# ScalarE issues the stores of the expert results, and SyncE runs on into the next layer's loads

## The chip, the cores and the metric

The kernel runs on one NeuronCore of one Trainium2 chip. The metric is the device time of one execution in microseconds (us), from three executions of the kernel before. Engines are called PE (TensorE, matrix products), DVE (VectorE), ACT (ScalarE), POOL (GpSimd) and SP (SyncE). SP computes nothing: it issues loads and stores to the 16 DMA engines. "PEq", "ACTq", "SPq" and "POOLq" are the sequencers of these engines, which issue DMAs and handle registers, branches and semaphores.

## What is computed

Two encoder layers over 512 tokens (two groups of 256) of width 1024, then a final norm. Of a layer only the second half matters here:

```python
h2 = rms_norm(x, norm_ffn) * (1 + scale2) + shift2
x = x + gate2 * grouped_moe(h2, w_router, router_bias, w_gate, w_up, w_down)

def grouped_moe(h, w_router, router_bias, w_gate, w_up, w_down):
    ...
    for e in range(N_EXPERTS):                      # 16 experts, 2 of them for each token
        a = jax.nn.silu(t @ w_gate[e]) * (t @ w_up[e])
        out = out + gate[:, e:e + 1] * (a @ w_down[e])
```

The first half of a layer starts with the modulation `silu(c) @ w_ada`, a norm of x, and the projection with `w_in`. All values are fp32.

## The kernel before

**The expert stage.** Each token's row is copied to a DRAM buffer (`rows_by_expert`) at the places of its two experts. The buffer is cut into tiles of 128 rows that belong to one expert. In this run each layer has 16 tiles. They are handled in pairs (`par` 0 and 1): a hardware loop over 7 pairs (`rest`), and a last pair written out behind it. For each tile, three weights of 2 MB (gate, up, down) and 0.5 MB of rows are loaded, and a result of 0.5 MB (`y_row[:, par, :]`) is stored back to its place in the buffer. The weights live in six slots of SBUF (`ring0` to `ring5`), three for each `par`. A product is made in three passes: ACT writes a rounded copy of half a weight (`high`, L1291, 128x2048), DVE subtracts it from the weight (`low`, L1835), and PE multiplies high by high, high by low and low by high (L943 to L945 for gate and up, L958 to L960 for down). Such a half weight is a "part"; six parts make a tile, and the semaphore `part_used` counts the parts that PE has finished.

**The order on each engine is written out by hand.** On PE, tile n takes: turning the next tile's rows (L923), its own two up parts, the next tile's first gate part, turning its own activations (L931), the next tile's second gate part, and its two down parts. L931 waits for DVE's product of silu and up (L1861). On ACT, tile n takes: the next tile's rows rounded (`rows_high`, L1298), silu (L1312), the next tile's second gate part, two down parts, the turned activations rounded (L1319), two up parts, the first gate part of the tile after the next, and last the two copies of the result from PSUM to `y_row` (L1328), which raise `y_ready`. Then the next tile's L1298 follows.

**SP.** For each tile `expert` (L638 on) loads the rows and the three weights of the tile two further on, each as soon as `part_used` says that its slot has been used up. The last load, of down, waits for the tile's last part. Then SP waits for `y_ready` and issues the store (L648). Behind both last tiles SP waits until the stores have landed (`y_stored`) and raises `tiles_stored`. Only then does SP enter the next pass of the layer loop.

**Between the layers.** POOL waits for `tiles_stored` (L1940), then gathers the rows from the buffer with 8 indirect DMAs (L1943). All engines meet at a barrier (`arrived`, `go`) which POOL's arrival completes. In the new layer, SP loads in the order of `BLOCKS`: `ada0`, `ada1`, `qa` (2 MB in 8 DMAs of 256-byte pieces), `ada2`, `ada3`, and so on. For the first block in each slot it waits for a count of `part_used` that says when the slot's last expert weight was used (L585); `LAST_PARTS` holds how many parts before the stage's end that is: 12 for `ada0`, 8 for `ada1`, 4 for `qa`, 6 for `ada2`, 0 for `ada3`. Before the load of `ada3` it waits until the gather is complete. PE multiplies `ada0` and `ada1` (L716), ACT copies the products (L1125) and then weighs the gathered rows (L1091), DVE adds the second expert's rows (L1508), PE turns the sums (L748), and DVE adds them to x (L1500). Behind the second layer the same steps L1091 to L1500 follow, without any load of weights.

Of the kernel before, what the change touches and what calls it, by code (L numbers as in the profile page):

```python
# [29 lines left out]
P = 128  # L30
# [6 lines left out]
DEPTH = 2  # L37
# [15 lines left out]
MAX_TILES = 2 * TOK // P + NE  # L53
# [35 lines left out]
PARTS_BEFORE = 16  # L89
# [209 lines left out]
def build_trunk(nc, t_in, y_prompt, y_sample):  # L299
# [7 lines left out]
    with ctx:  # L307
# [3 lines left out]
        def sem(name):  # L311
            return ctx.enter_context(nc.semaphore(name))


        rows_dram = nc.dram_tensor("rows_by_expert", (TILE_ROWS, D), F32, kind="Internal").ap()
# [51 lines left out]
        y_row = part(10240, 2048).rearrange("p (b d) -> p b d", b=2)  # L367
# [47 lines left out]
        plan_i = sb("plan_i", [1, 4 + MAX_TILES], I32)  # L415
# [18 lines left out]
        S = {n: sem(n) for n in names}  # L434
# [7 lines left out]
        xg_landed = [sem(f"xg_landed{par}") for par in range(2)]  # L442
        rows_sent = sem("rows_sent")
        rows_out = sem("rows_out")
        tiles_stored = sem("tiles_stored")
        got_rows = [sem(f"got_rows{t}") for t in range(TT)]
        arrived = sem("arrived")
        go = sem("go")
# [2 lines left out]
        passed = sem("passed")  # L451
        xgT_done = sem("xgT_done")
# [4 lines left out]
        part_used = sem("part_used")  # L457
# [5 lines left out]
        y_ready = sem("y_ready")  # L463
        y_stored = [sem(f"y_stored{par}") for par in range(2)]
# [73 lines left out]
        def _(sp):  # L538
# [36 lines left out]
            with sp.Fori(0, DEPTH) as layer:  # L575
# [39 lines left out]
                def expert_of(tile):  # L615
                    return sp.value_load(plan_i[0:1, bass.ds(tile + 4, 1)], min_val=0, max_val=NE - 1)

                def load_weights(k, e, par):
                    name = ("w_gate", "w_up", "w_down")[k]
                    sp.dma_start(ring[EXPERT_SLOTS[par][k]][:, :].rearrange("p (k n) -> p k n", k=(KC, KC, FC)[k]),  # L620
                                 t_in[name][bass.ds(layer, 1), bass.ds(e, 1), :, :]
                                 .rearrange("o e (k p) n -> p (o e k) n", p=P))\
                      .then_inc(w_landed[par][k], 16)

                def load_rows(tile, par):
                    sp.dma_start(xg[:, par, :], rows_dram[bass.ds(tile * P, P), :]).then_inc(xg_landed[par], 16)
# [6 lines left out]
                load_rows(0, 0)  # L633
                load_rows(1, 1)

                def expert(p, par, last=False):
                    n = (done_before + p) * 2 + par
                    tile = p * 2 + par  # L638
                    at = (done_before + p) * 12 + 2 + 6 * par
                    if not last:  # L640
                        e = expert_of(tile + 2)
                        sp.wait_ge(xgT_done, n + 1)
                        load_rows(tile + 2, par)
                        for k, after in enumerate((0, 2, 6)):
                            sp.wait_ge(part_used, PARTS_BEFORE + at + after)
                            load_weights(k, e, par)
                    sp.wait_ge(y_ready, n + 2)
                    sp.dma_start(rows_dram[bass.ds(tile * P, P), :], y_row[:, par, :]).then_inc(y_stored[par], 16)  # L648

                with sp.Fori(0, rest) as p:  # L650
                    for par in range(2):
                        expert(p, par)
                for par in range(2):
                    expert(rest, par, last=True)
                for par in range(2):
                    sp.wait_ge(y_stored[par], (done_before + rest) * 16 + 32)
                nc.sync.sem_inc(tiles_stored, 1)

            for t in range(TT):
                sp.wait_ge(y_rows_a, t + 1)  # L660
# [358 lines left out]
        def _(act):  # L1019
# [109 lines left out]
            with act.Fori(0, DEPTH) as layer:  # L1129
# [172 lines left out]
                def expert(p, par, last=False):  # L1302
# [24 lines left out]
                    for half in range(2):  # L1327
                        ins = nc.scalar.copy(y_row[:, par, half * 512:(half + 1) * 512], bank[2 + half][:, :])  # L1328
                    ins.then_inc(y_ready, 1)

                for h in range(2):
                    high(0, 0, 0, h, h, before * 12 + h)
# [568 lines left out]
        def _(pool):  # L1901
# [6 lines left out]
            with pool.Fori(0, DEPTH) as layer:  # L1908
# [26 lines left out]
                pool.wait_ge(rows_sent, layer * (32 * TT) + 32 * TT)  # L1935
                nc.gpsimd.sem_inc(rows_out, 1)

                pool.wait_ge(tiles_stored, layer + 1)
                nc.gpsimd.sem_inc(passed, 1)
                nc.gpsimd.drain().then_inc(arrived, 1)  # L1940
                for t in range(TT):
# [32 lines left out]
```

## Time and profile before

| | us |
|---|---|
| median of 3 runs | 1858.26 |
| lowest, highest | 1854.97, 1861.24 |
| the profiled execution, its own time | 1855.56 |
| its span, first to last instruction | 1853.7 |
| PE busy, DVE busy, ACT busy | 1525.7, 1042.1, 884.7 |

Around the span lie 1.9 us. The profiled execution is 2.7 us faster than the median. The busy times are sums over stages with different limits. The two expert stages run from about 558 to 912 us and from about 1452 to 1803 us.

### The profile page before, as it was taken

Reading aid. Unit: us, or ns where it says so; the run is one execution under the profiler, and the core shown is the slowest. Engines: PE = TensorE matmul, PEld = TensorE weight load, DVE = VectorE, ACT = ScalarE, POOL = GpSimd, SP = SyncE. Lnnn points to the kernel's source line nnn. Section 1 sums busy time; section 2 is a strip of 40 time slices with the busy share of each in tenths; the row PEclk is TensorE's granted clock in tenths of the full one; section 3 lists DMA queues with packets and bytes.
Section 4 is the critical chain, followed back from the end, with each engine's and each line's share of the span. In section 5 each row is a group of like instructions: output and inputs, shape, how many; then the busy total and the mean of one; then the engine's idle time right before and its main releaser. Section 6 shows DMA issues by size and latency. Waiting matters only on the chain.

```text
span 1853.7 us, 18702 instructions
## 1 busy us (share of the span) xinstructions
PE 1525.7 (82%) x6462; PEld 1090.4 (59%) x6462; DVE 1042.1 (56%) x1320; ACT 884.7 (48%) x1146; POOL 46.7 (3%) x45
## 2 busy tenths in 40 slices
PE   4799987999836999999569999699995389999974
PEld 2377545666614777777337664366672277777753
DVE  2654468223345777777353735932245387777744
ACT  2532357112225777777254324721123377777743
POOL 2001000000010000000100000000000000000001
PEclk9899998999967999999779999899997699999996
DMA  8629660112246999999392147011123789899933
GB/s 244 210 91 354 224 194 1 46 58 79 84 182 223 342 351 355 347 358 358 128 332 91 68 159 251 23 46 46 46 91 120 276 319 358 322 353 355 359 124 134
DMA packets 169107, 375.27 MB, mean 202 GB/s; under 512 B 22438, under 2 KB 25136, under 8 KB 168912
## 3 DMA queue, kind: packets, MB, share of 16 engines
q1 hardware_dynamic: 157792, 339.75, 51.3%
q0 software_dynamic: 8176, 31.46, 4.6%
q10 hardware_dynamic: 3072, 3.19, 0.6%
q8 instruction: 38, 0.62, 0.1%
q14 instruction: 29, 0.24, 0.0%
HBM read 333.49 MB, written 40.89 MB: 202 GB/s over the span
## 4 chain that ended last, share of the span: by engine, by line
PE 54%; DMA 15%; ACT 9%; issue 9%; DVE 8%; SPq 2%; ACTq 1%; POOL 1%; DVEq 0%; POOLq 0%
DMA ring<-in_w_gate 10%; PE bank L685 8%; PE bank L687 8%; PE bank L686 8%; PE bank L880 6%; PE bank L716 2%; PE bank L958 2%; PE bank L960 2%; PE bank L959 2%; PE bank L833 2%; PE bank L855 2%; PE bank L943 2%; PE bank L944 2%; ACT x_lo L1291 2%; PE bank L945 2%
## 5 line engine op out<-in xcount | busy, mean ns | idle before, releaser
L685 PE MATMUL bank<-x_hi,w_lo 128*128 128x512 f32 x608 | 259.2, 426 | 20.7 <-DVE x_lo L1448 9.0
L1291 ACT CAST x_lo<-ring 128x2048 fp32r<-128x2048 f32 x96 | 183.5, 1913 | 123.2 <-issue 56.8
L687 PE MATMUL bank<-x_hi,w_hi 128*128 128x512 f32 x608 | 239.9, 394 | 0.0
L686 PE MATMUL bank<-x_lo,w_hi 128*128 128x512 f32 x608 | 239.3, 394 | 0.0
L1835 DVE TENSOR_TENSOR w_lo<-ring,zone_r 128x2048 fp32r<-128x2048 f32 x92 | 210.4, 2289 | 28.3 <-ACT zone_r L1291 28.2
L1291 ACT CAST zone_r<-ring 128x2048 fp32r<-128x2048 f32 x96 | 181.6, 1912 | 19.9 <-PE bank L960 14.3
L943 PE MATMUL bank<-w_lo,zone_r 128*128 128x512 f32 x384 | 164.9, 429 | 5.2 <-issue 5.2
L685 PEld LDWEIGHTS bank<-x_hi,w_lo 128*128 128x128 f32 x608 | 115.5, 190 | 63.3 <-issue 30.2
L1425 DVE TENSOR_TENSOR w_lo<-ring,w_hi 128x1024 fp32r<-128x1024 f32 x84 | 102.0, 1220 | 85.1 <-ACT w_hi L1084 84.5
L1835 DVE TENSOR_TENSOR w_lo<-ring,x_lo 128x2048 fp32r<-128x2048 f32 x36 | 82.4, 2292 | 113.4 <-ACT x_lo L1291 113.4
L686 PEld LDWEIGHTS bank<-x_lo,w_hi 128*128 128x128 f32 x608 | 116.0, 191 | 31.7 <-issue 9.6
L687 PEld LDWEIGHTS bank<-x_hi,w_hi 128*128 128x128 f32 x608 | 115.6, 190 | 25.5
L1247 ACT ACTIVATE zone<-bank 128x512 f32<-128x512 f32 x32 | 19.1, 597 | 217.8 <-PE bank L687 217.8
L880 PE MATMUL bank<-zone,ring 128*128 128x512 f32 x256 | 115.8, 595 | 0.9
L944 PE MATMUL bank<-x_lo,zone_r 128*128 128x512 f32 x272 | 115.5, 425 | 0.0
L945 PE MATMUL bank<-x_lo,zone_r 128*128 128x512 f32 x272 | 114.9, 422 | 0.0
L1084 ACT CAST w_hi<-ring 128x1024 fp32r<-128x1024 f32 x84 | 87.1, 1044 | 22.4 <-PE bank L687 6.1
L923 PE MATMUL bank<-const,zone 128*128 128x128 f32 x256 | 35.0, 282 | 74.3 <-DMA zone<-rows_by_expert 74.3
L945 PE MATMUL bank<-zone_r 128*128 128x512 f32 x240 | 94.6, 394 | 0.0
L944 PE MATMUL bank<-zone_r 128*128 128x512 f32 x240 | 94.6, 394 | 0.0
L943 PEld LDWEIGHTS bank<-w_lo,zone_r 128*128 128x128 f32 x384 | 78.3, 204 | 22.4 <-issue 6.0
L1835 DVE TENSOR_TENSOR w_hi<-ring,x_lo 128x2048 fp32r<-128x2048 f32 x32 | 73.3, 2293 | 26.4 <-ACT x_lo L1291 26.4
(242 smaller groups left out, 2590.8 us busy)
## 6 DMA issues: line engine op xcount, KB each, us to landing
ring<-in_w_gate SPq DMA_DIRECT2D x32, 2048.0 KB, 13.5
ring<-in_w_up SPq DMA_DIRECT2D x32, 2048.0 KB, 15.7
ring<-in_w_down SPq DMA_DIRECT2D x32, 2048.0 KB, 8.8
ring<-in_w_ada SPq DMA_DIRECT2D x24, 2048.0 KB, 9.1
ring<-in_w_in SPq DMA_DIRECT2D x14, 2048.0 KB, 7.9
zone<-rows_by_expert SPq DMA_DIRECT2D x32, 512.0 KB, 8.7
rows_by_expert<-zone SPq DMA_DIRECT2D x32, 512.0 KB, 8.7
rows_by_expert<-zero_row POOLq DMA_DIRECT2D x4, 3072.0 KB, 28.8
```

Source lines behind the costliest of these rows:

```text
L685: mm(out, lo, x_first, start=start, stop=False)
L686: mm(out, hi, x_second, start=False, stop=False)
L687: return mm(out, hi, x_first, start=False, stop=stop)
L716: ins = mm(ps[32 * j:32 * (j + 1), :], cs[:, k, :], w[:, k, :], start=(k < 4), stop=(k >= KC - 4))
L880: ins = mm(ps[:, :], w[:, k, j * P:(j + 1) * P], oT[:, k, :], start=(k == 0), stop=(k == 3))
L943: mm(out, xg_hi[:, par, c, :], wv[:, c, :], start=(c == 0), stop=False)
L944: mm(out, xg_lo[:, par, c, :], hi[:, k, :], start=False, stop=False)
L945: ins = mm(out, xg_hi[:, par, c, :], hi[:, k, :], start=False, stop=(c == KC - 1))
L1084: nc.scalar.copy(w_hi[:, n % W_BUFS, :, :], group_view(ring[SLOT[b]], b, c)).then_inc(S["w_hi_ready"], 1)
L1291: nc.scalar.copy(part_hi[buf], ring[EXPERT_SLOTS[par][k]][:, h * 2048:(h + 1) * 2048])\
L1425: v.tensor_tensor(group_view(w_lo[SLOT[b]], b, c), group_view(ring[SLOT[b]], b, c), w_hi[:, n % W_BUFS, :, :].bitcast(F32), ALU.subtract). ...
L1835: v.tensor_tensor(w_low[EXPERT_SLOTS[par][k]][:, cols], ring[EXPERT_SLOTS[par][k]][:, cols], part_hi[buf].bitcast(F32), ALU.subtract)\
```

## The change

ACT itself waits for `y_ready` behind its two copies and issues the store. SP no longer waits for `y_ready`, issues no store, and has no pass for the two last tiles, since they had nothing but the store. SP also no longer waits for `y_stored`. POOL waits for both `y_stored` semaphores, with the number of pairs read from the plan, before it gathers. Nothing else is changed.

```diff
                 def expert(p, par):
...
-                    if not last:
-                        e = expert_of(tile + 2)
...
+                    e = expert_of(tile + 2)
+                    sp.wait_ge(xgT_done, n + 1)
+                    load_rows(tile + 2, par)
+                    for k, after in enumerate((0, 2, 6)):
+                        sp.wait_ge(part_used, PARTS_BEFORE + at + after)
+                        load_weights(k, e, par)
-                    sp.wait_ge(y_ready, n + 2)
-                    sp.dma_start(rows_dram[bass.ds(tile * P, P), :], y_row[:, par, :]).then_inc(y_stored[par], 16)
...
-                for par in range(2):
-                    expert(rest, par, last=True)
-                for par in range(2):
-                    sp.wait_ge(y_stored[par], (done_before + rest) * 16 + 32)
-                nc.sync.sem_inc(tiles_stored, 1)
...
                     for half in range(2):
                         ins = nc.scalar.copy(y_row[:, par, half * 512:(half + 1) * 512], bank[2 + half][:, :])
                     ins.then_inc(y_ready, 1)
+                    act.wait_ge(y_ready, n + 2)
+                    nc.scalar.sem_inc(passed, 1)
+                    act.dma_start(rows_dram[bass.ds((p * 2 + par) * P, P), :], y_row[:, par, :])\
+                       .then_inc(y_stored[par], 16)
...
-                pool.wait_ge(tiles_stored, layer + 1)
+                pool.wait_ge(S["plan_ready"], 1)
+                pairs_done = pool.value_load(plan_i[0:1, 1:2], min_val=0, max_val=DEPTH * MAX_TILES // 2)
+                for par in range(2):
+                    pool.wait_ge(y_stored[par], pairs_done * 16 + 16)
                 nc.gpsimd.sem_inc(passed, 1)
```

On ACT, at the end of the loop's second tile, before (the buffer `zone` is `y_row` at L1328, `bank2` and `bank3` hold the result, L1337 is the loop's branch):

```order
L1325 REGISTER_ALU
L1328 COPY zone<-bank2 128x512 [waits y_stored1,part_used]
L1328 COPY zone<-bank3 128x512
L1337 REGISTER_ALU
L1337 COMPARE_AND_BRANCH
L1296 ISA
L1298 CAST zone_r<-bank4 128x512 [waits xgT_done]
```

and now, at the same place, where the lines are 5 to 9 lower:

```order
L1316 REGISTER_ALU
L1319 COPY zone<-bank2 128x512 [waits y_stored1,part_used]
L1319 COPY zone<-bank3 128x512
L1323 ISA [waits y_ready]
L1323 DMA rows_by_expert<-zone 128x1024
L1332 REGISTER_ALU
L1332 COMPARE_AND_BRANCH
L1287 ISA
L1289 CAST zone_r<-bank4 128x512 [waits xgT_done]
```

A wait for the copies and a DMA now stand between the copies and the branch, and so ahead of all that ACT does for the next tile.

On SP, from the last load in the loop to the end of the layer loop (L575), before:

```order
L620 DMA ring5<-in_w_down 128x4x1024 [waits part_used]
L647 REGISTER_ALU
L648 ISA [waits y_ready]
L648 DMA rows_by_expert<-zone 128x1024
L650 REGISTER_ALU
L650 COMPARE_AND_BRANCH
L647 ISA
L648 ISA [waits y_ready]
L648 DMA rows_by_expert<-zone 128x1024
...
L575 REGISTER_ALU [waits y_stored0,y_stored1]
L575 COMPARE_AND_BRANCH
```

and now:

```order
L619 DMA ring5<-in_w_down 128x4x1024 [waits part_used]
L646 REGISTER_ALU
L646 COMPARE_AND_BRANCH
L574 REGISTER_ALU
L574 COMPARE_AND_BRANCH
```

The branch of the layer loop follows the last load of down directly, with no wait between.

## Rows read from the trace of the kernel before

**Rows 1.** Windows: stretch, its length, then PE, PEld, DVE, ACT, POOL busy, clock, DMA share.

```profile
700.00:800.00 100.00, 90.33 (x399) 72.85 (x397) 74.63 (x47) 75.30 (x64) 0.00 (x0) 0.95 0.95 355
881.00:909.00 28.00, 22.83 (x93) 17.60 (x92) 13.96 (x10) 11.13 (x11) 0.00 (x0) 0.94 0.06 23
```

**Rows 2.** Timeline, one even tile: start, duration, engine, line [idle before <- releaser].

```profile
644.13 1.07 ACT L1328 COPY zone<-bank 128x512 f32<-128x512 f32 x2 [0.74 <-PE bank L960]
...
645.09 1.09 ACT L1298 CAST zone_r<-bank 128x512 fp32r<-128x512 f32 x2
...
648.50 2.29 DVE L1835 TENSOR_TENSOR w_lo<-ring,zone_r 128x2048 fp32r<-128x2048 f32 x1 [1.00 <-ACT zone_r L1291]
```

**Rows 3.** Timeline, PE's wait for DVE: the stage's first tile, an even, an odd.

```profile
593.60 0.66 PE L931 MATMUL bank<-const,root 128*128 128x128 f32 x4 [1.63 <-DVE root L1861]
...
653.65 0.66 PE L931 MATMUL bank<-const,root 128*128 128x128 f32 x4 [0.39 <-DVE root L1861]
...
675.17 0.66 PE L931 MATMUL bank<-const,root 128*128 128x128 f32 x4 [3.35 <-DVE root L1861]
```

**Rows 4.** Timeline, the end of an odd tile: ACT's gate cast, PE's last product, the copies.

```profile
661.02 1.91 ACT L1291 CAST x_lo<-ring 128x2048 fp32r<-128x2048 f32 x1 [1.98 <-DMA ring<-in_w_gate]
...
662.20 0.40 PE L960 MATMUL bank<-x_lo,zone_r 128*128 128x512 f32 x1
...
662.84 1.06 ACT L1328 COPY zone<-bank 128x512 f32<-128x512 f32 x2
663.91 1.28 ACT L1298 ACT_TABLE_LOAD   x1
```

**Rows 5.** One line's instructions: SP's store, ACT's loads of x (ns min/median/max).

```profile
L648 SPq DMA_DIRECT2D rows_by_expert<-zone x32: 332/368/387, 603.9 to 1800.3; - x32
...
L1048 ACTq DMA_DIRECT2D zone<-in_x_prompt x2: 455/797/1139, 14.6 to 15.8; - x2
L1048 ACTq DMA_DIRECT2D zone<-in_x_sample x2: 473/617/761, 16.2 to 16.7; - x2
```

**Rows 6.** Chain that ended last, 602 to 650 us: SP's store, ACT's loop branch.

```profile
603.71 0.06 SPq L648
...
604.26 0.05 issue
...
621.37 0.06 ACTq L1337
621.43 0.21 issue
```

**Rows 7.** Timeline, the end of the first expert stage and the next layer's start.

```profile
890.88 1.07 ACT L1328 COPY zone<-bank 128x512 f32<-128x512 f32 x2 [3.65 <-PE bank L960]
...
908.92 0.33 SPq L648 DMA_DIRECT2D rows_by_expert<-zone  x1
...
915.14 28.03 SPq L571 DMA_DIRECT2D ring<-in_w_in  x8
...
938.16 3.64 PE L716 MATMUL bank<-ring,cs 128*32 128x512 f32 x16 [8.26 <-DMA ring<-in_w_ada]
...
942.72 4.27 ACT L1091 ACTIVATE zone<-zone,gw 128x1024 f32<-128x1024 f32 x4 [0.27 <-ACT tmp L1125]
...
949.90 6.36 DVE L1500 SCALAR_TENSOR_TENSOR xT<-bank,mod,xT 128x256 f32<-128x256 f32 x16 [1.12 <-PE bank L748]
```

**Rows 8.** Timeline, the same steps behind the second layer.

```profile
1800.25 0.33 SPq L648 DMA_DIRECT2D rows_by_expert<-zone  x1
...
1825.52 6.36 DVE L1500 SCALAR_TENSOR_TENSOR xT<-bank,mod,xT 128x256 f32<-128x256 f32 x16 [0.57 <-PE bank L748]
```

**Rows 9.** Windows: the clock behind PE's waits of 1.63 us (593.60) and 3.35 us (675.17).

```profile
594.00:595.00 1.00, 1.00 (x7) 0.85 (x6) 1.00 (x1) 0.71 (x2) 0.00 (x0) 1.00 1.02 381
...
676.00:678.00 2.00, 2.00 (x6) 1.60 (x5) 1.92 (x2) 2.00 (x2) 0.00 (x0) 0.50 1.06 391
678.00:680.00 2.00, 2.00 (x8) 1.57 (x6) 1.71 (x1) 0.25 (x1) 0.00 (x0) 0.68 1.05 387
```

More of the change, by code:

```diff
@@ L444, in build_trunk @@
         rows_out = sem("rows_out")
-        tiles_stored = sem("tiles_stored")
         got_rows = [sem(f"got_rows{t}") for t in range(TT)]
@@ L634, in _, with expert @@
                 load_rows(1, 1)
-                def expert(p, par, last=False):
+                def expert(p, par):
                     n = (done_before + p) * 2 + par
@@ L639, in expert @@
                     at = (done_before + p) * 12 + 2 + 6 * par
-                    if not last:
-                        e = expert_of(tile + 2)
[L642 to L646, printed above, removed]
-                    sp.wait_ge(y_ready, n + 2)
-                    sp.dma_start(rows_dram[bass.ds(tile * P, P), :], y_row[:, par, :]).then_inc(y_stored[par], 16)
+                    e = expert_of(tile + 2)
[4 more added lines that the diff above has]
+                        load_weights(k, e, par)
                 with sp.Fori(0, rest) as p:
```

## Prediction

> **What bounds the kernel now.** The busy times in the table above show no full engine: PE, the busiest, works 1525.7 of 1853.7 us. So the stages have to be looked at one by one. The change touches the two expert stages and the passage between the layers. In the middle of an expert stage the windows show PE at 90%, DVE and ACT at 75% and the DMA engines at 0.95 [rows 1]. Everything is nearly full there, so the question is which wait ends last.
>
> The timeline of one tile answers it [rows 2, 3]. ACT's copies of the result start at 644.13, after waiting for PE's last down product. Then ACT works without a gap: rows rounded at 645.09, then silu, then a gate part. DVE has waited 1.00 us for that part and starts on it at 648.50. At the end of DVE's work stands its product of silu and up, and PE waits 0.39 us for it at L931. Only then can PE do the second gate part and the down parts, whose end releases the next copies. So a tile is one serial chain: PE's end, ACT's copies, ACT's casts, DVE, PE. Odd tiles have the same chain, longer by two table loads, and PE waits 3.35 us there [rows 3]. **What ACT does between its copies and the first cast is on the path in every tile.** ACT's average of 75% hides that.
>
> Beside it runs a DMA chain. The load of down is issued at PE's end, rows and the next gate weight queue behind it, and in odd tiles ACT waits for that gate weight (1.98 us at 661.02) before its copies [rows 4]. PE's last product ended at 662.60 and the copies started at 662.84; the even tile's copies started as soon as PE was done. So the DMA chain ends only some 0.2 us later than the PE chain.
>
> **Part 1: SP loses the wait for y_ready and the store.** SP's next gate load goes out a little earlier, but it queues behind the 2 MB of down, which are issued at the same moment as before. The bytes between that issue and the gate's landing are the same 5 MB (down 2, store 0.5, rows 0.5, gate 2), whichever queue the store sits on, and the DMA engines are at 0.95 [rows 1]. I count nothing.
>
> **Part 2: ACT gains a wait and a store in every tile.** Behind the copies ACT must (a) see its own last copy finished, (b) raise a semaphore, (c) compute the address and issue the DMA; only then comes the next tile's L1298. For (c) the nearest row is the same store on SP, 603.71 to 604.31, 0.60 us in all [rows 6], of which the DMA itself is 0.37 [rows 5]. For (a) and (b) it is ACT waiting for its own copy (L1125), raising a semaphore and going on: 0.27 us idle [rows 7]. Today L1298 starts 0.11 us before the copies end (645.09 against 645.20) [rows 2], and this overlap is lost as well. 0.60 + 0.27 + 0.11 is 0.98. As both rows hold one start of an operation, some 0.08 us, I take **0.90 us for an even tile**. In an odd tile the loop's branch, 0.06 and 0.21 us [rows 6], ran under the copies and now comes behind the DMA, while where a table load follows there was no overlap to lose (663.91, 0.01 us behind the copies) [rows 4]. I take **1.10 us for an odd tile**.
>
> Who waits for it: L1298, silu, the gate cast, then DVE, then PE at L931, without slack, as shown above. In each stage 16 tiles store, and 15 of them have a tile behind: 8 even, 7 odd. 8 x 0.90 + 7 x 1.10 = 14.9 us a stage, **+29.8 us** for both. The lower bound: if waits and address vanish under the copies and only the DMA and the lost overlap are seen, 0.37 + 0.11 = 0.48 us a tile, 14.4 us. The upper: if a store from ACT costs what ACT's loads of the same size cost (0.455 to 1.139, mean 0.71) [rows 5] instead of 0.37, 0.34 us more a tile, 40 us. I stay with SP's row, as it is the same store and ACT's loads stood among many small ones.
>
> What the loop gives back: in odd tiles the gate's landing comes 0.2 us too late today [rows 4]. It keeps its distance to the issue of down, while the even tile's PE chain grows by 0.9 us, so this lateness goes: 0.2 x 13 odd tiles, **-2.6 us**, between 0 and twice that.
>
> **Part 3: SP runs ahead into the next layer.** This is the gain. Today the DMA engines are at 0.06 from 881 to 909 us [rows 1], while PE works on the last two tiles. Only after the last store does SP issue ada0, ada1 and qa, and POOL gathers at the same time. PE gets ada1 at 938.16, ACT weighs the rows from 942.72, and DVE adds to x from 949.90 [rows 7], 40.98 us behind the issue of the last store. Behind the second layer the same steps run without loads and take 1825.52 - 1800.25 = 25.27 us [rows 8]. Now ada0 goes out right behind the last down load, ada1 when the up weight of the last tile but one is used up, qa when its down weight is, at 890.88 [rows 7], and ada2 behind qa. Three loads have 18 us ahead of the last store. What ends last is then the gather, as behind the second layer: 40.98 - 25.27 = **-15.7 us**. PE's products of ada0 and ada1 (3.64 us each) run while POOL gathers. Next in line is ada3, which still waits for the gather. PE wants it only after turning the sums, the norm's sums of squares and ada2's product; those cover a load of 2 MB. If that cover were gone, the gain would shrink by what the load is late.
>
> Not covered are qa's small pieces: issuing them takes 28.03 us beside the gather today [rows 7]. Begun at 891, their tail and ada2 may lie beside the last store and the first gathers. I count **+1.0 us**, between 0 and 6.
>
> **Part 4: POOL waits for y_stored itself.** Its register load comes early, while POOL has nothing to do. SP's step between landing and POOL goes: **-0.1 us** a layer.
>
> **The sum**, against the profiled execution's own 1855.56: 29.8 - 2.6 - 15.7 + 1.0 - 0.2 = +12.3 us. The median lies 2.7 us above that execution; on the median, 1858.26 + 12.3 = **1870.5 us**, 0.7% more. A measurement of this kernel can tell about 0.3% (5.6 us) from no change. With a cost of c us a tile the sum is 30c - 17.5: nothing at 0.58, 0.3% faster below 0.40, 0.3% slower above 0.77.
>
> **The rivals.**
> *ACT's wait and store are cheap, and the passage wins.* It decides at c below 0.40. At 0.3 the sum is -8.5, 1850 us. For it: the sequencer is apart from the engine, and a step may run under the copies. Against it: the DMA must stand behind the end of the last copy, and alone it takes 0.37 us on SP [rows 5].
> *Cost and gain cancel.* At 0.48, the lower bound, to 0.77 the sum is -3.1 to +5.6: 1855 to 1864 us. For it: steps (a) to (c) are read at different places and may overlap more than I allow.
> *The two issuers get in each other's way.* SP issues rows and gate within a microsecond or two of ACT's store. ACT's loads at the start, issued beside SP's, took 0.71 us in the mean [rows 5]; 30 x 0.34 is 10 us more, 1881 us. The Trainium skill (Perfetto Trace Analysis, "DMA Instruction — HWDGE (DVE, Sync)") describes a generator of descriptors that two sequencers share and lock, the wait for the lock counted in the DMA's profiled time. By that rule ACT's store would stretch whenever SP holds the generator, up to one more such DMA; no row here shows it apart from other causes.
> *PE's clock falls in even tiles too.* Behind PE's wait of 3.35 us the granted clock is 0.50, the lower level of 1.2 GHz, over 2 us, and 0.68 over the next 2; behind the wait of 1.63 us it is 1.00, 2.4 GHz [rows 3, 9]. An even tile's wait would be 0.39 + 0.9 = 1.3 us, below 1.63, which speaks against it. Price: 2 x 0.50 + 2 x 0.32 = 1.6 us in each of 16 even tiles, 25 us, 1895 us.
>
> **How the numbers follow.** The forecast (c from 0.77 to 1.15) 0.46; ACT is cheap 0.14; cancelling 0.22; the issuers collide 0.13; clock 0.05. Some of cancelling's upper edge and some of the forecast's lower edge may change places. Faster by over 0.3%: 0.14; within 0.3%: 0.24; slower: 0.62. The range reaches down to cancelling's lower end (1855) and up past the collision with 3 us more lost at qa (1884); the cheap case and the clock are left out.
>
> **What would show it.** Right: PE's idle time before L931 longer by 0.8 to 1.1 us in each tile; a pair of tiles 1.8 us longer; DVE's L1500 25 to 27 us behind the last store of the first stage. Wrong: L1298 starting within 0.5 us of the copies' end, a pair of tiles as long as before, or ada0 and ada1 landing only behind the last store.

## The result and the profile after

| | before | after |
|---|---|---|
| median, us | 1858.35 (4 runs) | 1876.99 (4 runs) |
| lowest, highest, us | 1854.97, 1861.24 | 1875.29, 1878.31 |
| the profiled execution's own time, us | 1855.56 | 1876.33 |
| its span, us | 1853.7 | 1874.2 |
| PE, DVE, ACT busy, us | 1525.7, 1042.1, 884.7 | 1542.5, 1042.4, 886.5 |

The changed kernel takes 18.6 us more: a ratio of 1.0098, with a 95% interval of 1.0077 to 1.0119. The forecast was 1870.5 us, slower by 0.7%. DVE and ACT do the same work in the same time. PE is busy 16.8 us longer with the same 6462 products, which already says that its clock took part.

All lines below the change move: the copies are L1319 now (L1328 before), the rows rounded L1289 (L1298), the part casts L1282 (L1291), PE's wait for DVE L922 (L931), x updated at L1495 (L1500). ACT's store is L1323.

**What stands behind the copies now.** The timeline of an even tile, the counterpart of [rows 2, 3], and of an odd one, the counterpart of [rows 3, 4] (start, duration, engine, line, and in brackets the idle time before and what ended it):

```profile
639.77 1.08 ACT L1319 COPY zone<-bank 128x512 f32<-128x512 f32 x2 [0.72 <-PE bank L951]
641.09 0.34 ACTq L1323 DMA_DIRECT2D rows_by_expert<-zone  x1
641.54 1.07 ACT L1289 CAST zone_r<-bank 128x512 fp32r<-128x512 f32 x2 [0.70 <-ACT zone L1319]
...
644.94 2.29 DVE L1830 TENSOR_TENSOR w_lo<-ring,zone_r 128x2048 fp32r<-128x2048 f32 x1 [1.00 <-ACT zone_r L1282]
...
650.09 0.66 PE L922 MATMUL bank<-const,root 128*128 128x128 f32 x4 [1.20 <-DVE root L1856]
...
659.07 1.07 ACT L1319 COPY zone<-bank 128x512 f32<-128x512 f32 x2 [0.65 <-PE bank L951]
661.07 1.28 ACT L1289 ACT_TABLE_LOAD   x1 [0.93 <-ACT zone L1319]
...
716.69 1.12 PE L922 MATMUL bank<-const,root 128*128 128x128 f32 x4 [3.72 <-DVE root L1856]
```

The copies end at 640.85, the DMA is issued from 641.09 to 641.43, and the cast follows at 641.54. Before, the cast started 0.11 us ahead of the copies' end; now it starts 0.70 us behind. So the step costs 0.81 us on ACT in an even tile. In an odd one ACT idles 0.93 us, where it idled 0.01, which is 0.92. PE's wait for DVE grew by exactly the even tile's 0.81 (0.39 to 1.20). In odd tiles it grew by less, from 3.15 to 3.60 us before to 3.68 to 3.72 us, because part of the delay shows earlier in the same step: PE's weight loads now stand still for 0.54 us ahead of the next tile's gate part (at 709.94, in the step that the copies at 703.43 open). In odd tiles the copies now also wait for PE (0.65): the 0.2 us by which the gate came too late in [rows 4] are gone.

**The store itself.** One line's instructions, as in [rows 5] (ns min/median/max):

```profile
L1323 ACTq FUSED_REGOPS  x32: 60/60/65, 596.7 to 1820.0; - x32
L1323 ACTq MOVE rows_by_expert<-zone x32: 29/29/29, 596.8 to 1820.0; - x32
L1323 ACTq DMA_DIRECT2D rows_by_expert<-zone x32: 338/347/404, 596.9 to 1820.1; - x32
...
DMA to landing us min/median/max: 2.6/8.0/8.7
```

347 ns on ACT against 368 ns on SP: the same instruction at the same price.

**From copies to copies.** The distance from one tile's copies to the next shows what a tile costs. Over the first stage (L1328 before, L1319 after):

| | before | after |
|---|---|---|
| 7 steps from an even tile's copies | 18.56 to 18.94 | 19.30 to 19.42 |
| 6 steps from an odd tile's copies, with table loads | 22.92 to 24.08 | 24.89 to 25.01 |
| the odd step out of the loop, the last step | 18.53, 16.79 | 19.50, 17.46 |
| first to last copies, first stage | 305.1 | 322.2 |
| the same, second stage | 303.8 | 322.1 |

An even step is one that an even tile's copies open, and so its store. Over both stages the even steps grow by 0.67 us in the mean, the odd ones by 1.91. That is twice 0.94: half of it is the store, the other half was not in the forecast.

**PE's clock behind the wait.** Windows of the kernel after in an odd tile, as in [rows 9] (columns as in [rows 1]; the number before the last two is the granted clock). PE's wait ended in the first of them:

```profile
672.00:674.00 2.00, 1.67 (x6) 1.58 (x7) 2.00 (x2) 0.52 (x2) 0.00 (x0) 0.50 1.05 388
674.00:676.00 2.00, 2.00 (x6) 1.52 (x6) 1.17 (x3) 1.86 (x2) 0.00 (x0) 0.50 1.05 387
676.00:678.00 2.00, 2.00 (x7) 1.52 (x6) 2.00 (x1) 0.00 (x0) 0.00 (x0) 0.50 1.05 385
678.00:680.00 2.00, 2.00 (x10) 1.65 (x9) 0.19 (x1) 1.55 (x1) 0.00 (x0) 0.97 1.06 391
```

The kernel before, in the window in which PE restarts (at 675.17), ahead of the two in [rows 9]:

```profile
674.00:676.00 2.00, 0.82 (x6) 0.76 (x7) 2.00 (x3) 0.13 (x1) 0.00 (x0) 0.96 1.04 384
```

So before, the clock stood at 0.96, 0.50 and 0.68 in the three windows from PE's restart on. Now it stands at the lower level, 1.2 GHz, from the restart to about 678. In even tiles, behind a wait of 1.20 us, it stays at 1.00.

**The passage between the layers**, the counterpart of [rows 7] and, in its last two lines, of [rows 8]:

```profile
882.71 5.45 SPq L572 DMA_DIRECT2D ring<-in_w_ada  x2
900.44 8.85 SPq L570 DMA_DIRECT2D ring<-in_w_in  x8
909.62 34.98 SPq L572 DMA_DIRECT2D ring<-in_w_ada  x2
...
919.02 0.34 ACTq L1323 DMA_DIRECT2D rows_by_expert<-zone  x1
...
925.46 6.40 PE L707 MATMUL bank<-ring,cs 128*32 128x512 f32 x32 [7.81 <-DVEq L1515]
925.76 0.97 POOL L1941 DMA_INDIRECT zone<-rows_by_expert,slot_i  x1 [384.78 <-remote]
...
940.97 1.15 ACT L1082 ACTIVATE zone<-zone,gw 128x1024 f32<-128x1024 f32 x1 [4.31 <-POOLq L1946]
...
946.97 6.36 DVE L1495 SCALAR_TENSOR_TENSOR xT<-bank,mod,xT 128x256 f32<-128x256 f32 x16 [0.57 <-PE bank L739]
...
1820.10 0.35 ACTq L1323 DMA_DIRECT2D rows_by_expert<-zone  x1
1845.29 2.83 DVE L1495 SCALAR_TENSOR_TENSOR xT<-bank,mod,xT 128x256 f32<-128x256 f32 x7 [0.57 <-PE bank L739]
```

SP has issued `ada0`, `ada1`, `qa` and `ada2` 9 us before the last store. PE starts its 32 products as soon as the barrier opens. From the store to L1495 it takes 27.95 us instead of 40.98, and the last to come is the gather (ACT waits for POOL at 940.97). Behind the second layer the distance is 25.19 us, as before (25.27).

### The profile page after: what moved, and what is told of

Its sections match the earlier page's. It is cut to its first block, busy times and chain, and to the rows that moved or that the text cites. A ratio compares the mean times of both kernels' runs of the same rounds, so it can differ in the third digit from the quotient of the medians.

```text
span 1874.2 us, 18722 instructions
## 1 busy us (share of the span) xinstructions
PE 1542.5 (82%) x6462; PEld 1099.7 (59%) x6462; DVE 1042.4 (56%) x1320; ACT 886.5 (47%) x1146; POOL 48.0 (3%) x45
## 4 chain that ended last, share of the span: by engine, by line
PE 62%; ACT 11%; DVE 9%; issue 8%; DMA 5%; ACTq 1%; POOL 1%; SPq 1%; DVEq 0%; POOLq 0%; another core or an unknown queue 0%
PE bank L676 8%; PE bank L678 8%; PE bank L677 8%; PE bank L871 6%; PE bank L949 3%; PE bank L951 3%; PE bank L950 3%; PE bank L934 3%; PE bank L935 3%; PE bank L936 3%; PE bank L707 2%; DVE x_hi L1830 2%; PE bank L824 2%; PE bank L846 2%; ACT x_lo L1282 2%
## 5 line engine op out<-in xcount | busy, mean ns | idle before, releaser
L1282 ACT CAST x_lo<-ring 128x2048 fp32r<-128x2048 f32 x96 | 181.8, 1913 | 117.3 <-issue 57.8
L1830 DVE TENSOR_TENSOR w_lo<-ring,zone_r 128x2048 fp32r<-128x2048 f32 x92 | 210.4, 2289 | 28.4 <-ACT zone_r L1282 28.3
L1282 ACT CAST zone_r<-ring 128x2048 fp32r<-128x2048 f32 x96 | 181.0, 1906 | 19.9 <-PE bank L951 14.4
L934 PE MATMUL bank<-w_lo,zone_r 128*128 128x512 f32 x384 | 170.4, 444 | 6.7 <-issue 5.2
L1238 ACT ACTIVATE zone<-bank 128x512 f32<-128x512 f32 x32 | 19.1, 597 | 217.3 <-PE bank L678 217.3
L935 PE MATMUL bank<-x_lo,zone_r 128*128 128x512 f32 x272 | 119.2, 438 | 0.0
L936 PE MATMUL bank<-x_lo,zone_r 128*128 128x512 f32 x272 | 118.0, 434 | 0.0
```

Source lines behind the costliest of these rows:

```text
L934: mm(out, xg_hi[:, par, c, :], wv[:, c, :], start=(c == 0), stop=False)
L935: mm(out, xg_lo[:, par, c, :], hi[:, k, :], start=False, stop=False)
L936: ins = mm(out, xg_hi[:, par, c, :], hi[:, k, :], start=False, stop=(c == KC - 1))
L1282: nc.scalar.copy(part_hi[buf], ring[EXPERT_SLOTS[par][k]][:, h * 2048:(h + 1) * 2048])\
L1830: v.tensor_tensor(w_low[EXPERT_SLOTS[par][k]][:, cols], ring[EXPERT_SLOTS[par][k]][:, cols], part_hi[buf].bitcast(F32), ALU.subtract)\
```

## The experiments

Each kernel was timed beside the kernel before on the same chip; ratios are to that. "Run-ahead" stands for SP's going on into the next layer's loads.

**1. Run-ahead alone.** SP stores the tiles of the loop as before; ACT stores only the last pair, so that SP can go on.

The edit to the changed kernel, SP's loop first, then ACT's:

```diff
+                    sp.wait_ge(y_ready, n + 2)
+                    sp.dma_start(rows_dram[bass.ds(tile * P, P), :], y_row[:, par, :]).then_inc(y_stored[par], 16)
...
+                    if last:
                         act.wait_ge(y_ready, n + 2)
...
```

> SP issues the stores of the looped tiles again, as before; ACT issues only the stores of each stage's last pair, so SP still runs ahead into the next layer's loads. My theory (the loss is ACT's wait and store between the copies and the next casts, the gain is the run-ahead): the loop's period goes back to 41.7 us a pair, only tile 14 still pays 0.8 us a stage, and the passage keeps its gain of about 11 us (13.0 up to L1500 less 2.1 in the cold sums of squares behind it): 1858 + 1.6 - 11 = 1849 us. Rival (running ahead itself costs what the change lost, for instance by loads beside the last tiles): 1865 to 1877.

Measured: 1850.79 us (1847.92 to 1852.32), ratio 0.9947 [0.9930, 0.9964], 9.9 us below the 1860.70 of the kernel before beside it, within 2 us of what I had expected (1849).

**2. ACT's stores alone.** The change, but SP waits at the end of the stage until the last stores have landed, as it did before.

```diff
 (the change, SP behind its loop)
+                for par in range(2):
+                    sp.wait_ge(y_stored[par], (done_before + rest) * 16 + 32)
+                nc.sync.sem_inc(sp_passed, 1)
```

> ACT issues all stores as in the change, but SP waits at the end of each stage until the last two stores have landed before it enters the next layer's loads. My theory: all of the loop's cost and none of the gain, 1858 + 35 = 1893 us, with DVE's L1500 again some 41 us behind the first stage's last store. Rival (the run-ahead gives nothing): 1877, as the change.

Measured: 1889.04 us (1886.09 to 1892.14), ratio 1.0153 [1.0126, 1.0180], 28.3 us more. In its stages the steps are those of the kernel after (19.30 to 19.42, and ten of the twelve odd ones 24.8 to 25.1). **The two halves add up**: -9.9 + 28.3 = +18.4, and the change as a whole measured +18.6.

**3. ACT stores the even tiles of the loop only** (and the last pair; SP the odd ones; run-ahead as in experiment 1).

```diff
-                    if last:
+                    if last or par == 0:
```

> As the run with ACT storing the last pair only, but in the loop ACT also issues the stores of even tiles (par 0); SP issues those of odd tiles. My theory: the chain behind an even tile's copies grows by 0.81 us, of which 0.2 is covered by the late gate weight, and PE's wait in the next tile stays short enough to keep its clock: 14 x 0.6 = +8.5 us over the last-pair run. Rival (a store on a second queue slows the weight loads, whichever tile it is from): half of the change's loss in each, +17 us.

Measured: 1847.05 us (1839.69 to 1851.92), ratio 0.9937 [0.9913, 0.9962]. I had expected 8.5 us over experiment 1, and there was none. A miss, and an instructive one. The profiled execution is the fastest of its six. Two of its PE waits, an odd and an even tile's:

```profile
670.23 0.66 PE L925 MATMUL bank<-const,root 128*128 128x128 f32 x4 [3.15 <-DVE root L1860]
...
689.59 0.66 PE L925 MATMUL bank<-const,root 128*128 128x128 f32 x4 [1.22 <-DVE root L1860]
```

and the windows around the first of them:

```profile
668.00:670.00 2.00, 0.00 (x0) 0.00 (x0) 2.00 (x2) 0.64 (x1) 0.00 (x0) 1.00 1.02 403
670.00:672.00 2.00, 1.77 (x10) 1.55 (x11) 2.00 (x2) 1.07 (x2) 0.00 (x0) 1.00 1.04 398
672.00:674.00 2.00, 2.00 (x11) 1.63 (x10) 1.62 (x3) 1.63 (x2) 0.00 (x0) 1.00 1.06 388
```

The even steps pay their price in full (19.31 to 19.43). But behind a wait of 3.15 us the clock stayed at 1.00 here, and six of the twelve odd steps take 21.35 to 21.37 us, against 22.6 to 24.1 before. In the same execution, behind another wait of 3.15 us, it was at the lower level for six us:

```profile
751.62 1.12 PE L925 MATMUL bank<-const,root 128*128 128x128 f32 x4 [3.15 <-DVE root L1860]
```

```profile
751.00:753.00 2.00, 1.38 (x6) 1.29 (x7) 2.00 (x2) 0.23 (x1) 0.00 (x0) 0.50 1.05 404
```

That odd step took 23.99 us. **So 21.36 us is an odd step with SP's store and no loss of clock, and the odd steps of the kernel before held 1.3 to 2.7 us of low clock each.** The mean of the twelve odd steps is 22.30 in this execution and 23.33 in that of experiment 1, 12.4 us won in all, while the fourteen even steps lost 7.4 us.

**4. ACT stores the odd tiles of the loop only.**

```diff
-                    if last:
+                    if last or par == 1:
```

> As the last-pair run, but in the loop ACT also issues the stores of odd tiles (par 1), which are followed by the loop's branch and the two table loads. My theory: 14 x 0.92 = 12.9 us of plain delay, and 12 to 14 times about 1.1 us because PE's wait grows from 3.3 to 4.2 us and its low clock then covers more of its work: +26 us over the last-pair run, three times the even run's. Rival (queues): +17 us.

Measured: 1862.75 us, ratio 1.0004 [0.9978, 1.0029], 12 us over experiment 1 where I had expected 26. Its ten times spread from 1850.38 to 1872.37, more than any other kernel's. In the trace the odd steps run from 22.27 to 24.87 us, in no order. 22.27 is 21.36 + 0.91: the store's price in an odd tile with no loss of clock. PE's wait in one of these steps, and the clock behind it:

```profile
759.78 0.66 PE L925 MATMUL bank<-const,root 128*128 128x128 f32 x4 [3.72 <-DVE root L1860]
```

```profile
760.00:762.00 2.00, 2.00 (x12) 1.71 (x11) 2.00 (x2) 1.53 (x2) 0.00 (x0) 1.00 1.06 389
```

The changed kernel has this same wait (3.68 to 3.72 us) in every odd tile of the loop, and loses 2.6 to 2.75 us behind each. The mean is 23.75, so the clock costs about 1.5 us a step here, no more than before (the traced execution, 1855.30 us, is one of the faster ones). In the median only the plain price shows, 12 x 0.92 = 11 us. What the clock takes depends on both kinds of tiles together, and the price of the whole is not the sum of even and odd: -3.7 us (experiment 3) and +12.0 us against experiment 1, but some +26 us for both together (the change). Why is not shown.

**5. The wait without the store.** The kernel before; ACT waits for `y_ready` and steps a semaphore, SP stores.

```diff
+                    act.wait_ge(y_ready, n + 2)
+                    nc.scalar.sem_inc(passed, 1)
```

> The kernel before, with only the wait for y_ready and the semaphore step added on ACT behind each tile's copies; SP still stores. It splits the price: of the 0.73 us that ACT now idles behind the copies, the issue of the DMA with its address is about 0.5, the wait about 0.2 plus the lost overlap of 0.1. My theory: +0.3 us in even tiles (0.2 of it hidden by the late gate weight) and +0.3 to 0.5 in odd ones, with some clock loss: 8 to 14 us, 1866 to 1872. Rival (a wait for one's own copy is free, the DMA is all of the price): 1858 to 1860.

Measured: 1869.47 us (1868.75 to 1872.52), ratio 1.0065 [1.0042, 1.0087]. Behind the copies ACT idles here as follows, first an even tile, then an odd one:

```profile
600.65 1.07 ACT L1298 CAST zone_r<-bank 128x512 fp32r<-128x512 f32 x2 [0.18 <-ACT zone L1328]
...
619.68 1.28 ACT L1298 ACT_TABLE_LOAD   x1 [0.43 <-ACT zone L1328]
```

So waiting for one's own copy costs 0.18 + 0.11 of lost overlap = 0.29 us in an even tile and 0.42 in an odd one, and the address and the DMA cost the other 0.5 us. Most of the 10.7 us lie in the odd steps (23.9 us in the mean instead of 23.1, 9.8 us for the twelve): wait and clock together.

**6. The store where ACT is idle anyway.** The change, but tile n's store is issued in tile n+1 behind its down casts. For that the first pair is written out ahead of ACT's loop.

```diff
+                    if not very_first:
+                        store(n - 1, p * 2 + par - 1, 1 - par)
...
-                    act.wait_ge(y_ready, n + 2)
-                    ...
+                    if ends_here:
+                        store(n, p * 2 + par, par)
...
-                with act.Fori(0, rest) as p:
+                expert(0, 0, very_first=True)
+                expert(0, 1)
+                with act.Fori(1, rest) as p:
```

> As the change, but ACT issues the store of tile n later, in the middle of tile n+1, behind the two casts of down, where it then idles some 2 us waiting for PE's turned activations; the last tile's store stays where it was. My theory: all of the loop's loss goes and the run-ahead stays: 1846 to 1849 us. Rival (the loss comes from the second queue or from SP's changed order, not from the place of the store on ACT): near the change, 1870 to 1877.

Measured: 1798.13 us (1796.11 to 1799.78), ratio 0.9672 [0.9646, 0.9699]. That is some 50 us less than I expected, so something else had changed as well. Its timeline around one tile:

```profile
638.80 1.08 ACT L1327 COPY zone<-bank 128x512 f32<-128x512 f32 x2
...
639.76 1.09 ACT L1289 CAST zone_r<-bank 128x512 fp32r<-128x512 f32 x2
640.71 0.64 ACT L1309 ACTIVATE tmp<-bank 128x512 f32<-128x512 f32 x1
...
645.39 0.34 ACTq L1296 DMA_DIRECT2D rows_by_expert<-zone  x1
...
648.32 0.66 PE L922 MATMUL bank<-const,root 128*128 128x128 f32 x4 [0.41 <-DVE root L1864]
...
655.88 1.91 ACT L1282 CAST x_lo<-ring 128x2048 fp32r<-128x2048 f32 x1 [2.17 <-DMA ring<-in_w_gate]
```

The cast starts ahead of the copies' end again, and the store lies where nobody waits for it. But also **no table load is left in the loop**: the kernel before has 14 at L1298 and 14 at L1312 (1283 ns each, one of each in all 7 passes of both layers), this one has 26 fewer in all (1120 ACT instructions instead of 1146). The compiler had set them at the head of the loop's body; with the first pair ahead of the loop it needs them only once. Experiments 9 and 10 split the two effects.

**7. Who brakes the passage?** Experiment 1, but `ada2` is loaded only when the gather is complete, as `ada3` is.

```diff
-                    if b == f"ada{ADA_FIRST - 1}":
+                    if b == f"ada{ADA_FIRST - 2}":
```

> As the last-pair run, but the load of ada2 waits until the gather is complete, as that of ada3 does; qa still runs ahead. My theory: the last store landed 1.9 us later and the gather took 0.8 us longer because ada2's 2 MB were in flight; both go, and ada2 still comes in time: DVE's L1500 25.5 us behind the last store instead of 28, 2 us faster than the last-pair run. Rival (qa's small pieces are what delays the store): no change there, and ada2 and ada3 may come too late, 0 to 4 us slower.

Measured: 1843.48 us (1837.70 to 1846.07), ratio 0.9920 [0.9893, 0.9947]. The passage itself did not change: from the last copies to x updated (L1498 in both) it takes 27.82 us here and 27.75 in experiment 1. I had expected 2 us less. The intervals of the two ratios overlap, so I read no gain from it.

**8. The clock by itself.** The change, and PE fills its odd wait with four products that nobody reads (eight instructions in the trace), so that it isn't idle there (`par == 0` on PE is the step that an odd tile's copies open). The kernel does more work than before, none is left out.

```diff
+                    if par == 0:
+                        for i in range(4):
+                            mm(bank[7][:, :], K("ident"), const[:, 0:512], start=True, stop=True)
                     turn_act(n)
```

> The change, with four extra products (ident by const, 128x512, into the unused bank7, read by nobody) on PE in each even tile, ahead of L922, where PE waits 3.7 us for DVE behind an odd tile's copies. They should fit into that wait. My theory: of the 25.0 us from an odd tile's copies to the next, 2.7 are PE working at its lower clock behind the wait; without an idle stretch the clock stays high, 22.3 us as in the fastest pairs of the odd-store run: 26 pairs' odd halves less 2.7 us each for 12 or 13 of them a layer, -32 us, 1842 to 1852 us. Rival (the low clock does not come from PE's idle stretch, or the extra work only delays PE): 1877 or more.

Measured: 1854.02 us (1849.69 to 1857.64), ratio 0.9964 [0.9946, 0.9983], 23 us below the change and a little faster than the kernel before, a little above the range I had given (1842 to 1852). In an odd step, the products and the wait that is left, then the windows around another such wait:

```profile
633.81 3.60 PE L977 MATMUL bank<-const 128*128 128x512 f32 x8
637.69 0.66 PE L922 MATMUL bank<-const,root 128*128 128x128 f32 x4 [0.28 <-DVE root L1859]
```

```profile
676.00:678.00 2.00, 2.00 (x6) 0.80 (x6) 2.00 (x2) 1.69 (x1) 0.00 (x0) 1.00 1.03 402
678.00:680.00 2.00, 1.72 (x8) 0.86 (x7) 2.00 (x3) 0.03 (x1) 0.00 (x0) 1.00 1.05 396
680.00:682.00 2.00, 2.00 (x10) 1.65 (x9) 2.00 (x2) 2.00 (x2) 0.00 (x0) 1.00 1.05 387
```

DVE delivers no earlier, and PE starts L922 no earlier; only the clock is different, 1.00 in these windows. All twelve odd steps now take 22.26 to 22.33 us instead of 24.9 to 25.05, and the even steps stay at 19.3. **So the low clock cost the changed kernel 2.68 us in each odd step** (24.98 against 22.30 in the mean), 32 us in all. Some 4 us of the gain go back in the last pair, whose odd step has no table loads and little wait to fill (21.44 us instead of 19.50, in both layers). That leaves 28 us in the steps, of which the medians show 23; in the two traces the first stage of this kernel starts 9.5 us later than that of the changed kernel, which is not explained either.

**9. The table loads by themselves.** The kernel before, with the first pair of ACT's loop written out ahead of it.

```diff
-                with act.Fori(0, rest) as p:
+                for par in range(2):
+                    expert(0, par)
+                with act.Fori(1, rest) as p:
```

> The kernel before, with only the first pair of ACT's loop written out ahead of the loop, so that the two table loads (1.28 us each) that stood at the head of ACT's loop body leave the loop. It asks how much of the late-store run's unexpected 1798 us comes from this side effect of its edit. My theory: 12 x 2.56 = 31 us of table loads and 12 to 13 times 1.6 us of low clock go, until the DMA chain binds at some 38 us a pair: 1858 - 44 = 1812 us, and the late store adds only the run-ahead's 10 us to that. Rival (the late place of the store made the gain): near 1858.

Measured: 1804.32 us (1798.16 to 1811.00), ratio 0.9721 [0.9677, 0.9765]: 56 us less, and 8 us less than I had expected. The odd steps fall from 23.1 us to between 18.53 and 20.36, 19.1 in the mean. Behind the first tile, PE's waits for DVE are 0.3 to 0.4 us in the odd steps and 0.4 to 2.2 us in the even ones, and the clock is 1.00 from 700 to 800 us. The table loads alone are 26 x 1.28 = 33 us; the low clock that experiment 3 lets one read in the kernel before, 12 x 1.71 = 20.5 us, is about the rest.

**10. The same on the changed kernel.**

> The change, with the same peeled first pair on ACT, the store staying directly behind the copies. It differs from the late-store run only by the store's place. My theory: with the table loads gone the loop is bound by the loads (ACT waits some 2 us for the gate weight in every tile of the late-store run), so most of the 0.8 us a tile is hidden: 1800 to 1806 us, 2 to 8 above the late-store run. Rival (the serial price stays whatever binds the loop): 30 x 0.85, 1823 us.

Its edit is that of experiment 9. Measured: 1818.68 us (1811.72 to 1823.67), ratio 0.9774 [0.9731, 0.9817]. I had expected the run-ahead to outweigh what is left of the store's price once ACT waits for loads anyway (1800 to 1806 us). It doesn't; the rival named there, 1823, was nearer. ACT in one tile:

```profile
639.90 1.91 ACT L1282 CAST zone_r<-ring 128x2048 fp32r<-128x2048 f32 x1 [1.30 <-DMA ring<-in_w_gate]
...
642.24 1.08 ACT L1319 COPY zone<-bank 128x512 f32<-128x512 f32 x2 [0.43 <-PE bank L951]
643.58 0.36 ACTq L1323 DMA_DIRECT2D rows_by_expert<-zone  x1
644.05 1.07 ACT L1289 CAST zone_r<-bank 128x512 fp32r<-128x512 f32 x2 [0.73 <-ACT zone L1319]
```

ACT waits 1.30 us for a weight and 0.73 us behind its copies, and the second costs nearly all the same: copies that start at PE's end are not shielded by a load that landed before. Windows of 700 to 800 us, experiments 9, 10 and 6:

```profile
700.00:800.00 100.00, 96.91 (x449) 78.14 (x448) 85.91 (x56) 74.97 (x63) 0.00 (x0) 1.00 1.04 395
```

```profile
700.00:800.00 100.00, 93.11 (x436) 75.38 (x435) 82.55 (x51) 72.63 (x63) 0.00 (x0) 1.00 1.03 377
```

```profile
700.00:800.00 100.00, 96.57 (x448) 77.84 (x447) 85.97 (x54) 75.06 (x64) 0.00 (x0) 1.00 1.03 390
```

With no loss of clock in any of them, these three show the plain price of the store: PE's share falls from 97% to 93% with the early store and is back at 97% with the late one. The stages of experiment 10 are 13.9 and 10.5 us longer than those of experiment 9 (291.0 against 277.1, 290.8 against 280.3), 24.4 us for 30 tiles, 0.81 us a tile in the mean. That it meets the 0.81 us read above is chance: an even step is 0.78 us longer, an odd one 0.52, and 5.2 us lie in the last steps of the two stages, which are short in experiment 9 (15.15 and 16.77 us). Experiments 10 and 6 differ in nothing but the place of the store, and by 20.5 us between the medians, 19 by the ratios: **0.6 to 0.7 us a tile for the early place over the late one**, with the clock at 1.00 from 700 to 800 us in both.

**11. The best version so far with `ada2` held back** (the edit of experiment 7 on experiment 6).

> The late-store run with ada2 held back until the gather is complete. Expected to be the fastest: 1798 less the 2 to 7 us by which holding ada2 beat the last-pair run, 1791 to 1796 us. Rival (holding ada2 gave nothing, the difference there was the scatter between runs): 1798.

Measured: 1795.61 us (1788.26 to 1802.35), ratio 0.9674 [0.9633, 0.9716]. It can't be told from experiment 6 (0.9672).

## Why the forecast was right, and what it lacked

The sign and the mechanism held: ACT pays in every tile, the passage wins, and the payment is larger. 12.3 us were forecast and 18.6 measured; the range (1855 to 1884) held it. Its terms were further off than its total: the loss of clock in odd tiles (11.6 us) was missing, the plain price in the tiles was put 3.4 us too high (by experiments 10 and 6, some 7 us or more), and the gain of the passage 3.9 us too high. That experiment 2 measures 28.3 us for ACT's stores, close to the 27.2 forecast, is in part luck, since the first two of these errors offset each other. Step by step:

**Part 2, the price in the tiles.** The chain was read rightly: what ACT does behind its copies goes to PE one for one (0.39 to 1.20 us). The size was a little high: 0.81 us instead of 0.90 in an even tile, 0.92 instead of 1.10 in an odd one. Of the signs named, PE's idle time before L931 was to grow by 0.8 to 1.1 us in each tile: it did in even tiles (0.81), not in odd ones (0.1 to 0.6, the rest shows ahead of the gate part). A pair of tiles was to take 1.8 us longer; it takes 2.6, which is the clock. The even steps grew by less still, 0.67 us, since part of the old even step was lost to other waits (18.53 to 18.94, where experiment 9 mostly shows 18.5). With 14 even steps at 0.67, 12 odd ones at 0.94 (22.30 - 21.36) and the last two steps of each stage (0.97 + 0.67 and 0.99 + 0.48) the plain price is 9.4 + 11.3 + 3.1 = 23.8 us. The forecast had 29.8 - 2.6 = 27.2. Experiments 10 and 6 give 19 to 20.5 for it.

**The clock, the missing term.** The forecast asked whether even tiles would fall to the lower clock (no, rightly: the wait became 1.20 us, below the 1.63 behind which [rows 9] show the clock at 1.00). It did not ask whether the loss in odd tiles would grow, and silently took it as fixed. It grew: with 21.36 us for a clean step, the twelve odd steps lost 1.71 us each before (mean 23.07) and 2.68 now. 12 x 0.97 = **11.6 us**. Together, 23.8 + 11.6 = 35.4 us is what the two stages grew by (17.1 + 18.3). The split rests on two clean steps: 21.36, seen six times in experiment 3, and 22.30, seen twelve times in experiment 8. That the clock falls behind these waits and that filling them keeps it up is shown. Why every odd tile of the changed kernel loses the full 2.7 us is not: the waits are 0.1 to 0.6 us longer than before, but in experiment 4 a wait of the same 3.72 us cost nothing, and in experiment 3 one of 3.15 us cost 2.6.

**Part 3, the passage.** -13.0 us from the store to x updated instead of -14.7. The cause named was right: the last to come is the gather. Short of it was the last store's landing, 4.5 us instead of the 2.6 behind the second layer, beside `ada2` on the DMA engines, and the gather came later by some 0.8 us. Then 2.2 us more go back: the products for the sums of squares (L748, before L757) take 9.62 us instead of 7.11, at a granted clock of 0.54 instead of 1.00 from 950 to 955 us, and the reciprocal of the norm starts at 959.91, 42.2 us behind the last copies, instead of at 960.71, 53.0 us behind them. Net -10.8 us. Experiment 1 (-9.9) and the difference between experiment 2 and the change (-12) agree with it. In the trace of experiment 1, which has the same loads in the passage, the store landed after 3.8 us and the reciprocal starts 40.2 us behind the last copies, 2 us earlier than here: so much varies with nothing changed there. Holding `ada2` back did not shorten the way to x updated (experiment 7, landing after 3.2 us), so what brakes the store is open.

**Part 4**, SP's step at the gather, is too small to be seen.

**The rivals.** *ACT cheap* fell: the idle time behind the copies is 0.70 us and more in every tile. *Cost and gain cancel* fell: 18.6 us, with an interval of 14 to 22. *The issuers collide* fell: ACT's stores took 338 to 404 ns although SP issued rows and gate within 1 us (641.22 and 641.83 beside 641.09). The Trainium skill (Perfetto Trace Analysis, "DMA Instruction — HWDGE (DVE, Sync)") lets one expect a wait for a shared generator inside such a time. Beside SP's loads of the loop no run shows one. The store of the last tile but one is different: it goes out while SP issues the eight DMAs of `qa`, and takes 0.40 us in the changed kernel (901.56) and 0.40 to 0.43 in experiments 1, 3, 4, 7 and 10, but 0.34 in experiment 2, where SP issues nothing beside it, and 0.34 in experiment 8, where it does. A wait for the generator would look so; it is not shown apart from other causes, and 0.06 to 0.09 us once a stage changes nothing in the sum. *Clock in even tiles* fell: behind their waits the clock stayed at 1.00. The mechanism it names did add a cost, but in the odd tiles, and half as large (11.6 us instead of 25).

**What stays open.** The traces of single executions don't close by themselves. In these two, the copies of the first stage start at 602.61 and at 595.54, 7.1 us apart, in code that neither the change nor an experiment touches; over all thirteen kernels they start between 595.5 and 605.1. Why they differ is not shown. The stages (+35.4), the passage (-10.8), that front (-7.1), the next layer's front (+2.3) and the tail (+0.7) make the +20.5 between the spans. Without the fronts it would be +25, outside the measured interval of 14 to 22 us. So either the changed kernel's earlier front is no accident, or the pair of traced executions overstates the stages. Experiment 2, where the passage gains nothing, speaks for the second: its median is 28.3 us higher, not 35.4. The 11.6 us for the clock and the 23.8 for the store are readings of these two traces, and may be some us too large.

## What to carry to other kernels

Before a wait or a DMA is given to an engine, read what stands behind its place in the order: directly behind a step that another engine releases, it cost 0.5 to 0.9 us in every tile here, although ACT was busy only 75% of the time; behind the casts, where ACT waits for data anyway, the same store cost too little to be told (4 us over both stages in the traces of experiments 6 and 9). Where PE already waits long enough for its clock to fall behind some of the waits, a change upstream is to be priced twice, once for the delay and once for the products that may then run at 1.2 GHz, and the costs of several edits need not add up. And look at what recurs in each pass of a hardware loop: two table loads at its head, 1.28 us each, cost 4 us a pass here with what they did to PE's clock, three times in all what the change was about.

## What the runs showed of the hardware

- **A wait of the same length costs nothing or 2.7 us.** Behind PE waits of 3.15 to 3.72 us the granted clock stayed at 1.00 in some odd tiles (3.15 in experiment 3, 3.72 in experiment 4) and fell to 0.50 for up to 6 us in others. The loss was mostly near 0, 1.5 or 2.7 us a step. The changed kernel had 2.6 to 2.75 in all twelve, other kernels drifted from one value to another, which may be why experiment 4 spread over 22 us; that was not tested. Filling the wait with products nobody reads kept the clock at 1.00 and gained 23 us.
- **A DMA costs ACT what it costs SP**: 0.35 us for the instruction, 0.09 for the address, and 0.2 to 0.4 for waiting on its own last copy.
- **Table loads**: 1283 ns, with the next cast 0.01 us behind, and placed at a loop's head in every pass. Writing the first pass out ahead of the loop removed 26 of 28 and 56 us, 33 us being the loads themselves; the rest is about what the low clock had cost (an estimate: 12 x 1.71 = 20.5 us).
- **Without the table loads the loads and PE are both nearly full**: 390 to 395 GB/s with a DMA share of 1.03 to 1.04 (experiments 6 and 9), against 355 before, and PE busy 97% of the time. Which of the two sets the pace was not separated. The Trainium skill (Perfetto Trace Analysis, "Roofline", its note on single-core kernels above 100% of HBM) lets one core draw more than its share of 358 GB/s when it is alone; these runs agree, with 109 to 110% of that.
